# A product-key expert stage: gathers of 32 tokens by 4 slots, sums in four column groups, and a ring of six places

## The reference

```python
q = (xb @ wq).reshape(PEER_BLOCK, PEER_HEADS, D_QUERY)   # 8 heads x 256, rms-normed
s1, s2 = q[..., :128] @ k1.T, q[..., 128:] @ k2.T
v1, i1 = lax.top_k(s1, 16)
v2, i2 = lax.top_k(s2, 16)
sv, si = lax.top_k(v1[..., :, None] + v2[..., None, :], 16)
expert = e1 * N_KEYS + e2          # the pair of keys behind each of the 16
g = jax.nn.softmax(sv, axis=-1)
act = jax.nn.gelu(jnp.einsum('phkd,pd->phk', jnp.take(u, expert, axis=0), xb))
out = jnp.einsum('phk,phkd->pd', g * act, jnp.take(v, expert, axis=0))
x = x + g2 * out;  y = rmsnorm(x, final_norm_w)
```

## Time and profile before

| what | before |
|---|---|
| median of 3 runs | 3307.72 us (3305.47 to 3307.90) |
| span of the profiled execution | 3302.0 us |
| busy: PE, DVE, ACT, POOL | 87%, 67%, 65%, 42% of the span |
| gathers on their DMA queue (q0) | 1118.5 MB, 82.1% of 16 engines |
| HBM over the span | 360 GB/s |

### The profile page before, as it was taken

The page is one execution under the profiler, slowest core; times in us unless marked ns, Lnnn a source line. Parts: engine busy times, 40 slices in busy tenths (PEclk is TensorE's granted clock), DMA queues, the critical chain, the costliest instruction groups (busy, mean ns, idle before and its releaser), DMA issues. The chain is left out here.

```text
span 3302.0 us, 33384 instructions
## 1 busy us (share of the span) xinstructions
PE 2886.4 (87%) x9454; PEld 1408.2 (43%) x9454; DVE 2218.7 (67%) x5274; ACT 2154.6 (65%) x7216; POOL 1392.2 (42%) x1135
## 2 busy tenths in 40 slices
PE   7999999888888888888898888888988898889886
PEld 5665455444434433444344344343443344434321
DVE  5687265776676667666766676667666766676665
ACT  3332143677777777777777777777777777777775
POOL 0000110455544555554455544544555445544553
PEclk9999999999999999999999999999999999999999
DMA  7232133999999999999999999999999999999997
GB/s 284 87 104 76 30 122 125 369 419 418 420 419 403 419 420 420 414 420 420 420 396 420 420 420 419 420 421 418 403 420 420 420 413 420 420 418 406 421 420 302
DMA packets 170079, 1190.91 MB, mean 361 GB/s; under 512 B 20058, under 2 KB 21498, under 8 KB 30242
## 3 DMA queue, kind: packets, MB, share of 16 engines
q0 software_dynamic: 155808, 1118.53, 82.1%
q1 hardware_dynamic: 14084, 70.23, 5.7%
HBM read 1179.42 MB, written 9.25 MB: 360 GB/s over the span
## 5 line engine op out<-in xcount | busy, mean ns | idle before, releaser
L929 PE MATMUL ps<-r_w,r_yT 128*128 128x512 f32 (+1 forms) x2712 | 1320.6, 622 | 256.2 <-ACT r_yT L1255 253.4
L604 POOL DMA_INDIRECT r_w<-in_peer_uv,gidx x678 | 860.5, 1269 | 880.3 <-PE ps L929 841.8
L1806 DVE SCALAR_TENSOR_TENSOR r_w<-r_w,r_qk 128x1024 f32<-128x1024 f32 x678 | 829.9, 1225 | 499.9 <-DMA r_w<-in_peer_uv,gidx 494.7
L929 PEld LDWEIGHTS ps<-r_w,r_yT 128*128 128x128 f32 (+1 forms) x2712 | 485.8, 192 | 1018.3 <-ACT r_yT L1255 600.8
L929 PE MATMUL ps<-r_yT 128*128 128x512 f32 (+1 forms) x904 | 443.7, 620 | 72.4 <-ACT r_yT L1255 70.1
L1247 ACT ACTIVATE mixc<-mixc 128x1 f32<-128x1 f32 x1056 | 207.8, 197 | 449.5 <-DVE r_w L1806 286.0
L1255 ACT ACTIVATE r_yT<-ident,mixc 128x128 f32<-128x128 f32 x1024 | 411.3, 402 | 33.2
L1252 ACT ACTIVATE mixc<-mixc 128x1 f32<-128x1 f32 x1056 | 408.9, 387 | 35.0
L1251 ACT ACTIVATE mixc<-mixc 128x1 f32<-128x1 f32 x1056 | 408.7, 387 | 33.8
L604 POOL DMA_INDIRECT r_yT<-in_peer_uv,gidx x226 | 298.5, 1321 | 269.4 <-PE ps L929 257.3
L1806 DVE SCALAR_TENSOR_TENSOR r_yT<-r_yT,r_qk 128x1024 f32<-128x1024 f32 x226 | 276.6, 1225 | 176.1 <-DMA r_yT<-in_peer_uv,gidx 175.9
(11 more groups left out here) (293 smaller groups left out, 2777.3 us busy)
## 6 DMA issues: line engine op xcount, KB each, us to landing
r_w<-in_ada_w SPq DMA_DIRECT2D x18, 1024.0 KB, 5.3
r_w<-in_peer_uv,gidx POOLq DMA_INDIRECT x678
r_w<-in_w_lin SPq DMA_DIRECT2D x16, 512.0 KB, 6.9
r_vo<-in_x_prompt SPq DMA_DIRECT2D x8, 512.0 KB, 7.2
r_qk<-in_ada_w SPq DMA_DIRECT2D x2, 2048.0 KB, 16.7
r_w<-in_w_out SPq DMA_DIRECT2D x2, 2048.0 KB, 8.9
r_w<-in_x_prompt SPq DMA_DIRECT2D x8, 512.0 KB, 3.5
x_dram<-r_w POOLq DMA_DIRECT2D x8, 512.0 KB, 3.4
```

The costliest lines, as they stand in the source:

```text
L604: pool.indirect_dma_start(ring[i], None, table, bass.IndirectOffsetOnAxis(gidx_t[:, h, j:j + 1], 0)).then_inc(e_ld[i], 16)
L929: mm = nc.tensor.matmul(ps[0:r, 2 * p + c, :], diag[:, j % 4, 0:r], row[:, D + c * 512:D + (c + 1) * 512], start=h == 0 and j == 0, stop=h ...
L1806: V.scalar_tensor_tensor(ring[i][:, 0:D], ring[i][:, 0:D], 1.0, h2[:, t, :], ALU.mult, ALU.mult, accum_out=dots[:, i:i + 1]).then_inc(dot_ ...
```

## The change

- **Slots.** A gather holds 4 slots each of 32 tokens, in place of one slot of 128. Partition 32k + j is token j of a quarter q of the tile, slot 4c + k. A quarter's token rows must then stand on all four groups of partitions: `replicate` (TensorE, a matmul with the 0/1 matrix `spread`) and `copy_rows` (ScalarE, 128x1024) make such rows (`xrep`) for each **build**. The order of slots is by sets of heads (`SETS`): from tile 2 on 4 heads, and within a set a quarter after the other, so a build holds for 16 slots.
- **Numbers and gates** of a head are turned to the new layout by `turn_places` and `turn_gates` (four small matmuls each) and copied out by Vector (`copy_places`) and ScalarE (`copy_gates`).
- **Mix.** Four matmuls of 32 columns (`sel32` scaled, 128x32) by 256 columns, one for each column group, sum the four slots and tokens together; a tile's sum is one [128, 4, 256] in banks 0 and 1, for all tiles, so the first mix of a tile waits for `acc_free`.
- **Ring.** Six places throughout.
- **Order.** Routes start at slots by a table (`ROUTE_AT`), from tile 2 on at slots 4, 20, 36... of a tile; six of them (`FAST`) in lumps of two pieces.
- **Final rows.** They are in that layout, so x1 and y move in four DMAs a tile each, of 1 KB pieces; the mean square needs a sum over column groups (`sum_squares` on TensorE, then `final_variance`).
- **ScalarE** has one small op fewer a slot (the factor of tanh moves into the dot), and its diagonal is 128x32.

```diff
-RING = 8
-PLACES = 11
+RING = 6
+PLACES = 6
...
+QUADS, NG = 4, 16
+QC = 256
+SETS = [((0,), (1,), (2, 3), (4, 5), (6, 7)), ((0, 1), (2, 3), (4, 5, 6, 7))] + [
+    ((0, 1, 2, 3), (4, 5, 6, 7))] * (NT - 3) + [((0,), (1,))]
+FAST = (2, 3, 12, 13, 14, 15)
+ROUTE_AT = {2: 2, 3: 10, 4: 22, 5: 37, 6: 53, 7: 69, 8: 85, 9: 101, 10: 116, 11: 132,
+            12: 146, 13: 154, 14: 162, 15: 170, 16: 180}
+ROUTE_AT.update({m: 180 + 16 * (m - 16) for m in range(17, (NT - 1) * HEADS + S_STEPS)})
+TURN_AT = (30, 38)
...
+        for t in range(NT):
+            for heads_of in SETS[t]:
+                for q in range(QUADS if t < NT - 1 else 1):
+                    builds.append((t, q))
+                    first.append(len(slots))
+                    for h in heads_of:
+                        for c in range(4 * q, 4 * q + 4) if t < NT - 1 else range(NG):
+                            slots.append((t, h, q, c, len(builds) - 1, number(t, heads_of[-1])))
...
+            def finish(t, nq, src, dst):
+                for c in range(4):
+                    sp.dma_start(x1s[c * DEC:(c + 1) * DEC, 0:nq, :],
+                                 src[:, c * QC:(c + 1) * QC].rearrange("(q j) n -> j q n", q=nq)).then_inc(x1_ld, 16)
                 sp.wait_ge(y_out, t + 1)
...
+            for n, (t, h, g, c, b, m) in enumerate(slots):
+                i = place[n]
+                if n == 0 or m != slots[n - 1][5]:
+                    pool.wait_ge(idx_ready, m + 1)
+                if uses[n] > 1 or i < RING:
+                    pool.wait_ge(v_free, RING + last_use[n] + 1)
...
+            def turn_places(m):
+                pe.wait_ge(idx_x, m + 1)
+                if m:
+                    pe.wait_ge(gate_ready, m)
+                for k in range(4):
+                    mm = nc.tensor.matmul(ps[k * DEC:(k + 1) * DEC, 6, 16:32], sel32, xi[:, :, k:NG:4],
+                                          start=True, stop=True)
+                mm.then_inc(idx_t, 1)
...
+            def replicate(b):
+                t, i = builds[b]
+                if b:
+                    pe.wait_ge(x_copy, b)
+                q = slice(i * DEC, (i + 1) * DEC)
                 for c in range(2):
-                    mm = nc.tensor.matmul(ps[0:r, 2 * p + c, :], diag[:, j % 4, 0:r], row[:, D + c * 512:D + (c + 1) * 512],
-                                          start=h == 0 and j == 0, stop=h == steps(r) - 1 and j == TOPK - 1)
+                    mm = nc.tensor.matmul(ps[:, 2 + c, :], spread[q, :],
+                                          h2[q, t, c * 512:(c + 1) * 512], start=True, stop=True)
+                mm.then_inc(x_rep, 1)
+            def mix(s):
+                t, h, q, _, _, _ = slots[s]
+                pe.wait_ge(dg_ready, s + 1)
+                if t and s == t * TILE_SLOTS:
+                    pe.wait_ge(acc_free, t)
+                row = ring[place[s]]
+                new, end = s == spans[t, q // 2][0], s == spans[t, q // 2][-1]
+                for c in range(4):
+                    mm = nc.tensor.matmul(ps[c * DEC:(c + 1) * DEC, q // 2, (q % 2) * QC:(q % 2 + 1) * QC], diag[:, s % 4, :],
+                                          row[:, D + c * QC:D + (c + 1) * QC], start=new, stop=end)
                 mm.then_inc(v_free, 1)
-            pe.wait_ge(kt_ld, 16)
+            def sum_squares(t, nq):
+                pe.wait_ge(f_sq, t + 1)
+                for c in range(4):
+                    mm = nc.tensor.matmul(ps[c * DEC:(c + 1) * DEC, 7, 0:nq], sel32, fss[:, 0:nq], start=True, stop=True)
+                mm.then_inc(f_mm, 1)
...
+            replicate(0)
+            for s in range(N_SLOTS):
+                t, j = slots[s][0], s - slots[s][0] * TILE_SLOTS
+                for m in routes(s):
+                    if s - ROUTE_AT[m] == 0 and m < number(NT - 1, 0):
+                        query(*tile_head(m), tile_head(m)[0] % 2)
+                b = build_at(s)
+                if b:
+                    replicate(b)
+                mix(s)
+                if s == 1:
+                    turn_places(1)
+                if s == 3:
+                    turn_gates(1)
+                for m in routes(s):
+                    if s - ROUTE_AT[m] == 2:
+                        scores(*tile_head(m))
+                    if s - ROUTE_AT[m] == piece(m) + 1:
+                        turn_places(m)
+                    if s - ROUTE_AT[m] == piece(m) + 3:
+                        turn_gates(m)
+                if t < NT - 2 and j in TURN_AT:
+                    turn(t + 1, TURN_AT.index(j), P)
+                if t and j == 4:
+                    sum_squares(t - 1, 4)
+            sum_squares(NT - 1, 1)
...
+                if s == 0 or m != slots[s - 1][5]:
+                    act.wait_ge(gate_ready, m + 1)
                 act.wait_ge(dot_done, s + 1)
...
-                nc.scalar.activation(kd[:, i:i + 1], d, ACT.Copy, scale=TANH_K)
...
+                act.wait_ge(v_free, RING + s - 3)
+                nc.scalar.activation(diag[:, s % 4, :], sel32, ACT.Copy,
...
+            def copy_rows(b):
+                act.wait_ge(x_rep, b + 1)
+                if b >= 2:
+                    act.wait_ge(dot_done, first[b - 1])
+                nc.scalar.activation(xrep[b % 2], ps[:, 2:4, :].rearrange("p b n -> p (b n)"), ACT.Copy).then_inc(x_copy, 1)
...
+            def copy_places(m):
+                t, h = tile_head(m)
+                dve.wait_ge(idx_t, m + 1)
+                V.tensor_copy(gidx_t[:, t % 2, h, :], ps[:, 6, 16:32]).then_inc(idx_ready, 1)
...
+            def dot(s):
+                i, b = place[s], slots[s][4]
+                if s == first[b]:
+                    dve.wait_ge(x_copy, b + 1)
                 dve.wait_ge(e_ld[i], 16 * uses[s])
+                V.scalar_tensor_tensor(ring[i][:, 0:D], ring[i][:, 0:D], TANH_K, xrep[b % 2], ALU.mult, ALU.mult,
...
+                dve.wait_ge(v_free, RING + (t * TILE_SLOTS + TILE_SLOTS if nq == 4 else N_SLOTS))
+                dve.wait_ge(g2_ld, 192)
+                V.tensor_tensor(a, ps[:, 0:2, :].rearrange("p b (q n) -> p (b q) n", q=2)[:, 0:nq],
+                                (g2b if nq == 4 else g2s).unsqueeze(1).broadcast_to([P, nq, QC]), ALU.mult).then_inc(acc_free, 1)
...
+                for q in range(nq):
+                    last = V.scalar_tensor_tensor(fdump, a[:, q], 1.0, a[:, q], ALU.mult, ALU.mult, accum_out=fss[:, q:q + 1])
+                    if q < nq - 1:
+                        fc.link(last)
+                last.then_inc(f_sq, 1)
+            def final_variance(t, nq):
+                dve.wait_ge(f_mm, t + 1)
+                V.tensor_scalar(frs[:, 0:nq], ps[:, 7, 0:nq], 1.0 / D, EPS, ALU.mult, ALU.add).then_inc(f_var, 1)
...
+            for s in range(N_SLOTS):
+                t, j = slots[s][0], s - slots[s][0] * TILE_SLOTS
+                dot(s)
+                if s == 1:
+                    scaled(NT - 1)
+                    route(1)
+                if s == 2:
+                    copy_places(1)
+                if s == 3:
+                    gates(1)
+                if t and j == 1:
+                    final_sum(t - 1, 4)
+                if t and j == 2:
+                    final_square(t - 1, 4)
+                if t and j == 5:
+                    final_variance(t - 1, 4)
+                if t and j == 9:
+                    final_scale(t - 1, 4)
```

448 lines of the change are left out of this document (222 added, 226 removed).

## The result

The changed kernel takes 3421.99 us (median of 4 runs, 3418.09 to 3425.36) against 3306.59 for the kernel before: ratio 1.0349, 95% interval 1.0334 to 1.0363. Slower, as forecast, but by 115 us where 53 were forecast and 95 was the range's upper end. The profiled execution spans 3423.6 us, 121.6 more than that of before; it is the slowest of its four and that of before the fastest, so some 6 us of the 121.6 are the choice of executions and not the change.

A forecast was written before the change was run, and what follows sets the result against it. DMA was taken to set the pace, through two engines about 10 us behind the other fourteen. Terms 36 + 6 + 5 + 7 + 3 + 0 - 4 = +53 us on a 3302.0 us span, 5.7 under the median, gave 3360; range 3314 to 3403.

The forecast's parts named there:

- What bounds the kernel: Gather stage: DMA sets the pace at 2.48 us a slot through two late engines; idle time of the other fourteen costs nothing.
- Two signs: Expected in the profile: tiles of some 325 us become 331 or so, and no dip is longer elsewhere.
- Six places, spare 5.0 and 4.5 us: Ring: a slot's chain may slip 5.0 us at TensorE's full clock, 4.5 at the lower, before the late engines run dry.
- The query of head 5, 36 us: Slot 4 of tiles 2 to 7: query with the sample's part slips mixes 11 us, losing 6 us in each of six tiles.
- Two such in tiles 0 and 1, 6 us: Queries with the sample's part inside tiles 0 and 1, with no final sum ahead: lose 3 us each.
- Other queries and fast routes, 5 us (0 to 25): Other queries slip a mix 2 to 4.3 us, under the spare; fast routes fill Vector in slots 146 to 185.
- The beginning, 3 us (0 to 10): First dot waits for first replication and row copy, about 602 for 594.8; full DMA queues absorb most, leaving +3 us.
- 1 KB rows, 7 us: Final rows: x1 and y in 1024 pieces of 1 KB a tile cost +7 us, bounds 0 to +60.
- The end, -4: After the last landing: work on 256 columns in place of 1024 takes 6.8 us in place of 10.6.
- Instructions, 0: More TensorE matmuls, fewer ScalarE ops: worth -5 to +10 us if an instruction queue feeds from a late engine, taken as 0.
- rival 1: Slips stay within the ring's spare: +6 us, or -2 with the pieces at line rate, about 3309 us; chance 0.13.
- Rivals 2 and 3: Faster by removing TensorE's backlog, 3286 us, chance 0.06; and column groups run one after the other, 3410 up, chance 0.04.

The follow-up runs named there:

- e14: Changed kernel with eleven places, the first replication and its row copy moved earlier, and the final sum behind slot 0's dot product: 3334.05 us.
- e2: Changed kernel, six places, with the sample's query joined to head 2's query in place of head 5's: 3417.76 us.
- e10: Changed kernel, six places, with the previous tile's final sum behind the dot product of slot 0 in place of slot 1: 3414.96 us.
- e7: Changed kernel, six places, with all replications after the first two left out on TensorE (it computes something else): 3401.49 us.
- e15: Changed kernel, six places, with two added 128x128 matmuls of zeros over 256 columns ahead of each mix: 3380.42 us.
- e6: Changed kernel with eleven places (eight and three that join later) and the sample's query at head 2: 3337.93 us.
- e13: Changed kernel, six places, with the first replication ahead of head 1's query and its row copy ahead of ScalarE's norm of the last rows: 3415.53 us.
- e4: Kernel before the change with six places in place of eight to eleven, nothing else changed: 3416.09 us.
- e5: Kernel before the change with x1 and y of each tile moved in four transfers of 256 columns, so 1 KB pieces: 3310.03 us.
- e12: Kernel before the change with seven places: 3323.07 us.
- e8: Changed kernel, six places, with two added small matmuls of zeros ahead of each mix around tile starts only, from tile 2 on: 3446.87 us.
- e3: Changed kernel, six places, with three added small matmuls (64 rows by 64 columns, zeros) ahead of every slot's mix: 4136.70 us.

## Why the prediction was right and wrong, by its own steps

**What bounds the kernel: right.** Idle time costs nothing while rows wait in the queues: with eight places GpSimd waits 7.81 us at a start that loses 3. The mix (0.64 to 1.08 for 0.8 to 1.3), the clock mostly at its lower level and the hole behind slot 4 are as written, with GpSimd waiting 9.43 us, a little under the "over 10". Two signs failed: a tile is 12 us longer and not 6, and there are dips elsewhere that matter, in tiles 0 and 1 (share 0.38 in tile 1, a GpSimd wait of 12.36 us in tile 0 where the kernel before has 9.80). That two particular engines set the pace was not tried.

**Six places, spare 5.0 and 4.5 us: right in form.** The start of a tile loses 9.6 us with six places, 5.2 with seven, 3.2 with eight and 2.2 with eleven (57.3, 31.4, 19.3 and 13.1 over six; the last is e14, with the early final sum). Less the 2.2 that eleven places leave: 7.4, 3.0, 1.0. The slip of 11 less spares of 4.5, 7.0 and 9.5 gives 6.5, 4.0, 1.5: the same order, each within 1 us, from a slip that the prediction worked out and no run measured by itself.

**The query of head 5, 36 us: right in mechanism, short in size.** Measured 57.3: 44 that places take away, as a slip's cost should, and 13 that stay at eleven places, which the sum did not have. The 57.3 hold all that a tile's first 32 slots lose; the sample's part is 26 of them (e2), the wait for the bank some 8 (e10).

**Two such in tiles 0 and 1, 6 us: the step that failed.** These tiles lost 41.3. The prediction counted the copies of rows on ScalarE and called them hidden; the replications that feed them, 3.78 us each on TensorE, it did not price. They stand there one in 4 or 8 slots, often just ahead of a query, and cost 20 us (e7). The sample's part costs some 4 us at each place it stands in tiles 2 to 7 (e2). With the clock up these tiles lose 27 (e15); this overlaps with the 20, since replications get shorter too. 15 to 16 us stay in these tiles at eleven places (e6, e14).

**Other queries and fast routes, 5 us (0 to 25): short.** 15.4 in the rest of tiles 2 to 7, within the bounds. The step that was off is "a query of 3.7 to 6 us slips a mix by 2 to 4.3 us, under the spare": at six places and the lower clock something goes past the spare here, at the full clock or with a seventh place it does not (-2.4 and -1.9).

**The beginning, 3 us (0 to 10): the first dot is 9.5 late, what that costs is open.** The prediction let full DMA queues absorb the later dot. e13's median speaks against it (6.5 less for a first dot 6.9 sooner), its profile for it (4.9 of the 6.9 lost again in tiles 0 and 1). Some 2.8 of the 9.5 may not be the change's: of the profiled runs of the kernel before's form, two (e4, e5) had their first dot at 597.7 and 597.6, one (e12) at 594.9.

**1 KB rows, 7 us: 3 in e5, open in the changed kernel.** Its own layout of the rows goes with 382 to 390 GB/s while they move, some 2 us a tile (e14), and e5 does not have that layout. **The end, -4: -2.9.** Instructions, 0: not told apart.

The sum's largest miss is thus tiles 0 and 1, 35 us, before the starts' 21. The range's upper end left no room for it: it took the bounds of queries and routes, but none for tiles 0 and 1. (With the bounds named, 48 and 25, the terms add up to 85 and not to the 95 written; and rival 1 with the pieces at line rate is -1, not -2.) Rival 1 (the spare holds) is nearly met with eight places, and still 33 us are lost there. Rivals 2 and 3 fell: it is slower, and TensorE is busy 6 tenths. What no forecast had is a cost of the change at any ring, 26 to 31 us: before the first dot 9 (2.5 with early rows), 15 to 16 in tiles 0 and 1, 12 to 13 at starts, 3 back at the end. From e6 to e14, with early rows, the early final sum and the sample's query back at head 5, 4 us went. At the starts it goes with a lower GB/s at a full DMA share while rows move, and not with a slip. What makes it in tiles 0 and 1 wasn't tried at eleven places: replications and that same row traffic are both candidates, and it stays open.

## What to carry to other kernels

In a ring, price a place by the longest stretch in which the consumer returns none: write down (places - 1) x transfer time, less the chain of one slot, and compare it with each slip. Places below that threshold are dear (the seventh was worth 93 us in the kernel before), those above it cheap (the next four 15 together). Apply the comparison first where the stages are densest (here the first two tiles), and count every engine that a helper step touches. When an engine is made much less busy, look whether it now runs at its lower clock just where its longest work stands.

## What the runs showed of the hardware that I had not expected

- A busy TensorE at half clock. In e8 it was busy 5.00 of 5.00 us in windows between 1640 and 1670 us while the granted clock was 0.50, with 64 x 64 matmuls and mixes of 32 columns; with two 128 x 128 matmuls of zeros a slot (e15) it was 0.8 or more in nearly every slice. With three of the 64 x 64 ones a slot (e3) it stood at 1.00 from 1740 to 1750 us and at 0.50 from 2070 to 2080, so these runs do not tell what decides between the levels. The Trainium skill (TensorE: Matmul & The Clock Gate, Part 1) says that an engine kept busy is released to full clock; these windows of e8 do not show that, and the measurement decides.
- Leaving out half of a query's matmuls did not shorten the queries (10.4 for 9.9 us), as the granted clock was still 0.50 through them.
- The same 155808 packets took longer with fewer places: 81.0% of 3423.6 us is 2773 us of all 16 engines, against 2711 before (82.1% of 3302.0) and 2775 in e4 (81.3% of 3412.8). At eleven places in the changed kernel, where the queues hardly ran dry, it is still 2736 (e6, 82.0% of 3336.1), more than before. So a DMA share near 1 does not say that the DMA moves what it can: it went with 420 GB/s before, with 400 to 413 between the dips of the changed kernel and with 382 to 390 while rows moved in e14.
